# Diagonal products in place of scaled transpositions, scalar steps on ScalarE, last additions on GpSimd and an earlier last tile, in a fused two-block transformer kernel

## The reference

```python
x = layer_norm(x, emb_ln_g, emb_ln_b)
mix = concat(y_a, y_b) @ w_out
x = layer_norm(ALPHA * x + gt1 * mix, ln1_g, ln1_b)
h = x * (1.0 + sc2) + sh2
f = (silu(gate) * up) @ w_ffn_out                 # 2816 hidden features
x = layer_norm(ALPHA * x + gt2 * f, ln2_g, ln2_b)  # end of the first block
u = rms_norm(x, norm_mix_pre) @ w_in_2             # second block
x = x + rms_norm(concat(o_nsa, o_conv) @ w_out_2, norm_mix_post)
h = rms_norm(x, norm_ffn_pre)
x = x + rms_norm((gelu(g) * up) @ w_ffn_down, norm_ffn_post)
```

## Time and profile before

| | |
|---|---|
| median of 3 runs | 1548.7 us (1545.46 to 1552.2) |
| the profiled execution | 1547.24 us, of which the span is 1545.4 us |
| mean granted TensorE clock | 0.956 of full speed |
| TensorE busy | 1418.1 us, 92% of the span |
| VectorE busy | 665.0 us, 43% |
| ScalarE busy | 548.5 us, 35% |
| GpSimd busy | 486.9 us, 32% |
| HBM traffic | 95 GB/s over the span |

### The profile page before, as it was taken

The page is one execution under the profiler, slowest core; times in us unless marked ns, Lnnn a source line. Parts: engine busy times, 40 slices in busy tenths (PEclk is TensorE's granted clock), DMA queues, the critical chain, the costliest instruction groups (busy, mean ns, idle before and its releaser), DMA issues.

```text
span 1545.4 us, 22772 instructions
## 1 busy us (share of the span) xinstructions
PE 1418.1 (92%) x9466; PEld 1166.4 (75%) x9466; DVE 665.0 (43%) x1199; ACT 548.5 (35%) x800; POOL 486.9 (32%) x132
## 2 busy tenths in 40 slices
PE   4899989899789999999987899999987999998996
PEld 1688767786678888878867878888777888887885
DVE  2555665353466333320046514687244544442003
ACT  2435534233242323221124244555355343432112
POOL 1333232014324444434331231111232444433341
PEclk9899999998889999999997798999999999999998
DMA  9652255002212232323322321101121223232211
GB/s 373 167 151 83 82 201 179 35 3 80 84 47 99 101 99 92 109 82 109 109 82 104 123 69 41 56 28 56 68 83 55 94 97 106 85 109 83 95 55 54
DMA packets 24596, 147.91 MB, mean 96 GB/s; under 512 B 2700, under 2 KB 3852, under 8 KB 8880
## 3 DMA queue, kind: packets, MB, share of 16 engines
q1 hardware_dynamic: 19152, 130.96, 24.0%
q10 hardware_dynamic: 5344, 15.51, 3.7%
HBM read 141.74 MB, written 4.72 MB: 95 GB/s over the span
## 4 chain that ended last, share of the span: by engine, by line
PE 77%; DVE 12%; ACT 4%; DMA 2%; POOL 2%; issue 2%; SPq 0%; ACTq 0%; DVEq 0%; POOLq 0%
PE bank L1974 20%; PE bank L1975 20%; PE bank L1976 20%; PE bank L2232 6%; POOL weight_lo L1254 2%; PE bank L1148 2%; DVE bank L1618 2%; DMA raw<-in_weights 2%; PE bank L1068 1%; ACT weight_hi L1293 1%; PE bank L2139 1%; PE bank L1139 1%; PE bank L1130 1%; DMA w<-in_w 1%; DVE xres L1615 1%
## 5 line engine op out<-in xcount | busy, mean ns | idle before, releaser
L1254 POOL TENSOR_TENSOR weight_lo<-raw,weight_hi 128x2048 fp32r<-128x2048 f32 (+1 forms) x98 | 445.6, 4548 | 881.0 <-ACT weight_hi L1293 880.9
L1974 PE MATMUL bank<-act_hi,weight_hi 128*128 128x512 f32 (+2 forms) x1136 | 437.4, 385 | 22.0 <-POOL weight_lo L1254 8.7
L1975 PE MATMUL bank<-act_lo,weight_hi 128*128 128x512 f32 (+2 forms) x1136 | 427.6, 376 | 0.0
L1976 PE MATMUL bank<-act_hi,weight_lo 128*128 128x512 f32 (+2 forms) x1136 | 427.3, 376 | 0.0
L1293 ACT ACTIVATE weight_hi<-raw 128x2048 fp32r<-128x2048 f32 (+1 forms) x98 | 185.1, 1890 | 414.1 <-PE bank L1976 406.1
L1974 PEld LDWEIGHTS bank<-act_hi,weight_hi 128*128 128x128 f32 (+1 forms) x1136 | 218.3, 192 | 64.6 <-issue 15.5
L1976 PEld LDWEIGHTS bank<-act_hi,weight_lo 128*128 128x128 f32 (+1 forms) x1136 | 217.9, 192 | 38.8
L1975 PEld LDWEIGHTS bank<-act_lo,weight_hi 128*128 128x128 f32 (+1 forms) x1136 | 218.5, 192 | 35.1
L1974 PE MATMUL bank<-weight_hi,hid_hi 128*128 128x512 f32 x352 | 141.0, 401 | 6.8 <-DVE acc L1618 4.7
L1975 PE MATMUL bank<-weight_lo,hid_hi 128*128 128x512 f32 x352 | 140.7, 400 | 0.0
L1976 PE MATMUL bank<-weight_hi,hid_lo 128*128 128x512 f32 x352 | 140.4, 399 | 0.0
(11 more groups left out here) (352 smaller groups left out, 1749.8 us busy)
## 6 DMA issues: line engine op xcount, KB each, us to landing
raw<-in_weights SPq DMA_DIRECT2D x120, 1024.0 KB, 4.8
w<-in_w ACTq DMA_DIRECT2D x2, 2048.0 KB, 10.9
bias_rows<-grow ACTq DMA_DIRECT2D x1, 2560.0 KB
xres<-in_x SPq DMA_DIRECT2D x4, 512.0 KB, 7.0
strip<-bias_rows ACTq DMA_DIRECT2D x1, 2048.0 KB, 9.2
out<-xres SPq DMA_DIRECT2D x4, 512.0 KB, 2.6
row_a<-in_ln_g ACTq DMA_DIRECT2D x2, 512.0 KB, 4.0
row_b<-in_ln_b ACTq DMA_DIRECT2D x2, 512.0 KB, 5.1
```

The source lines that it names most:

```text
L1254: pool.tensor_tensor(wlo[i % SPLIT][:, :size], raw[n % RAW][:, :size], whi[i % SPLIT][:, :size], ALU.subtract).then_inc(lo_ready, 1)
L1974: pe.matmul(o, l[0], r[0], start=first, stop=False)
L1975: pe.matmul(o, l[0], r[1], start=False, stop=False)
L1976: return pe.matmul(o, l[1], r[0], start=False, stop=last)
```

## The change

- **Filler order.** Tile 3 of `out1_0` is done after one more filler step, and tile 3 of `out1_1` after the remaining four. Each counts its unit as used right there; `dense_rows` skips the two units.
- **h3 and h4.** `xres` itself is multiplied by a diagonal matrix `diag` of the row scales (a plain product of 128 columns). ScalarE writes the 128 by 128 diagonal from the identity where it wrote the scaled tile. All three turns now wait tile by tile: eight feature groups of the first tile, then eight of the second.
- **Scalar steps.** Adding epsilon, scaling by 1/1024 and adding the two sums go into the bias and scale of ScalarE's root, or one small ScalarE step ahead of it. In h2 the offset is made by two small ScalarE steps. VectorE's steps for them are gone, and `inverse_x` of a tile stands between the halves of the next tile's normalisation.
- **Root early.** A root on a spare column stands ahead of `mix2` and of `ff2`.
- **The end.** VectorE multiplies into `acc` and GpSimd adds to `xres`, for all but the last half of the last tile. The last tile is stored in two halves.

```diff
+    last = [[("out1", n, TT - 1, k) for k in range(2)] for n in range(2)]
+    return order + begun[:1] + last[0] + begun[1:] + last[1] + [("norm", 2, 7), ("mixer", 2), ("norm", 3, 7), ("mixer", 3)]
...
+            first, second = squares[:, 2 * t:2 * t + 1], squares[:, 2 * t + 1:2 * t + 2]
+            a.step(act.activation(first, first, ACT.Identity, bias=eps[:, 1:2], scale=1.0 / DM))
+            a.done(act.activation(rstd[:, t:t + 1], second, ACT.Sqrt, bias=first, scale=1.0 / DM), S["rms_root"])
+
+        a.step(act.activation(eps[:, 3:4], eps[:, 2:3], ACT.Sqrt))
...
+            for x in between:
+                inverse_x(e + 1, x)
...
+        def last_rows(t):
+            dve.wait_ge(S["rms_root"], TT + t + 1)
+            d.step(V.reciprocal(rstd[:, t:t + 1], rstd[:, t:t + 1]))
+            if t >= 2:
+                dve.wait_ge(S["added"], 2 * (t - 1))
+            for j in range(2):
+                name, h = ("ff2", t, j), slice(SEQ * j, SEQ * j + SEQ)
+                if (t, j) == (TT - 1, 1):
+                    stt(bank(name)[:], bank(name)[:], rstd[:, t:t + 1], row4[:, h], ALU.mult, ALU.mult)
+                    tt(xres[:, t, h], xres[:, t, h], bank(name)[:], ALU.add, sem=drain(name, "dve"))
+                else:
+                    at = DM * (t % 2) + SEQ * j
+                    stt(acc[:, at:at + SEQ], bank(name)[:], rstd[:, t:t + 1], row4[:, h], ALU.mult, ALU.mult, sem=drain(name, "dve"))
...
+        for t in range(TT):
+            for j in range(2):
+                if (t, j) != (TT - 1, 1):
+                    h, at = slice(SEQ * j, SEQ * j + SEQ), DM * (t % 2) + SEQ * j
+                    await_drained(pool, ("ff2", t, j), "dve")
+                    o.step(pool.tensor_tensor(xres[:, t, h], xres[:, t, h], acc[:, at:at + SEQ], ALU.add), S["added"])
...
+        def normalise_row(t):
+            m, r = mv[:, t, 0:1], rstd[:, t:t + 1]
+            a.step(act.activation(m, m, ACT.Copy, scale=-1.0))
+            act.wait_ge(S["inverse1"], t + 1)
+            a.step(act.activation(m, m, ACT.Copy, scale=r))
+            a.done(act.activation(xres[:, t, :], xres[:, t, :], ACT.Identity, bias=m, scale=r), S["xn_ready"])
...
-            a.done(act.activation(xn2[:, t, :], xres[:, t, :], ACT.Copy, scale=x_sums[:, t:t + 1]), S["xn3_ready"])
+            a.done(act.activation(diag[:, t, :], ident[:], ACT.Copy, scale=x_sums[:, t:t + 1]), S["xn3_ready"])
...
-                early = begun is not None and n < len(begun)
-                weights = begun[n] if early else next_unit(f"{unit}_{n}")[0]
+                if begun is not None and n < len(begun):
+                    continue
+                weights = next_unit(f"{unit}_{n}")[0]
...
+                for k in range(KC):
+                    at, x = HALF * (k % 2) + P * t, source[:, 2 * half + t, P * k:P * k + P]
+                    o = bank((stage, half, k // 2))[:, at:at + P]
+                    if stage == "h2":
+                        mm = pe.transpose(o, x, ident[:])
+                    else:
+                        mm = pe.matmul(o, x, diag[:, 2 * half + t, :], start=True, stop=True)
+                    if t and k % 2:
+                        fill((stage, half, k // 2), mm)
...
+            mm = rows_product("mix1", n, 4, begun[n], (act_hi, act_lo), t, k)
+            if (t, k) == (TT - 1, 1):
+                mm.then_inc(unit_used, 1)
```

More of the change, by code:

```diff
@@ L843, in second_act, with second_dve @@
                 act.dma_start(row4[:], src["ffn_post"].partition_broadcast(P)).then_inc(load["rows4"], 16)
-        for s in range(TT + 1):
-            squares_of_rows("ff2", 1, s, rms_t2)
-    def second_dve(dve, d, ts, tt, stt, affine_lo_half, x_mean_square, inverse_x):
+                a.step(act.activation(eps[:, 3:4], eps[:, 2:3], ACT.Sqrt))
+        for t in range(TT):
+            squares_of_rows("ff2", 1, t, rms_t2)
+    def second_dve(dve, d, ts, tt, stt, affine_lo_half, inverse_x):
         V = dve
@@ L1004, in second_dve, with add_rms @@
             tt(act_lo[:, k, :], bank(("turn_o", k))[:], act_hi[:, k, :].bitcast(F32), ALU.subtract, sem=drain(("turn_o", k), "dve"))
-        def mean_square(stage, t):
-            for j in range(2):
-                await_drained(dve, (stage, t, j), "act")
-            tt(rstd[:, t:t + 1], squares[:, 2 * t:2 * t + 1], squares[:, 2 * t + 1:2 * t + 2], ALU.add)
-            ts(rstd[:, t:t + 1], rstd[:, t:t + 1], 1.0 / DM, RMS_EPS, ALU.mult, ALU.add, sem=S["rms_ready"])
-        def add_rms(stage, e, t, row):
+        def add_rms(stage, e, t, row, between=()):
             dve.wait_ge(S["rms_root"], TT * e + t + 1)
@@ L1050, in second_dve @@
         dve.wait_ge(load["rows4"], 16)
-        for s in range(TT + 1):
-            if s < TT:
-                mean_square("ff2", s)
-            if s:
-                add_rms("ff2", 1, s - 1, row4)
+        for t in range(TT):
+            last_rows(t)
     def second_pe(pe, three, next_unit, dense_feature, dense_token, dense_rows, dense_halves, fill):
@@ L1181, in finish @@
     def finish(sp):
-        for t in range(TT):
-            await_drained(sp, ("ff2", t, 1), "dve")
+        for t in range(TT - 1):
+            sp.wait_ge(S["added"], 2 * t + 2)
             sp.dma_start(out[0, tok(t), :], xres[:, t, :]).then_inc(load["out"], 16)
-        sp.wait_ge(load["out"], 16 * TT)
+        t = TT - 1
+        sp.wait_ge(S["added"], 2 * t + 1)
+        sp.dma_start(out[0, tok(t), 0:SEQ], xres[:, t, 0:SEQ]).then_inc(load["out"], 16)
+        await_drained(sp, ("ff2", t, 1), "dve")
+        sp.dma_start(out[0, tok(t), SEQ:DM], xres[:, t, SEQ:DM]).then_inc(load["out"], 16)
+        sp.wait_ge(load["out"], 16 * (TT + 1))
     @block.sync
@@ L1665, in _ @@
         d.step(V.memset(grow[:, SEQ:], -NEG), S["future_ready"])
+        for n, value in enumerate((LN_EPS, RMS_EPS, 1.0)):
+            d.step(V.memset(eps[:, n:n + 1], value))
         d.step(V.memset(restart[:], 1.0))
@@ L1945, in second_norm @@
                 stt(b, b, mv[:, t, 0:1], row2_a[:, h], ALU.subtract, ALU.mult)
+            for x in between:
+                inverse_x(0, x)
             for j, h in enumerate(halves):
@@ L2059, in dense_rows @@
                     order = [(t, k) for t in range(TT) for k in range(2)]
-                elif n == 0 or early:
-                    tiles = (TT - 1,) if early else range(TT)
-                    order = [(t, k) for k in range(2) for t in tiles]
                 if ready is not None and n in ready:
@@ L2091, in turn_half @@
                 pe.wait_ge(ready[0], ready[1] + 2 * half + t + 1)
-            for i in range(KC // 2):
-                for k in (2 * i, 2 * i + 1):
-                    for t in range(2):
-                        at = HALF * (k % 2) + P * t
-                        mm = pe.transpose(bank((stage, half, i))[:, at:at + P], source[:, 2 * half + t, P * k:P * k + P], ident[:])
-                fill((stage, half, i), mm)
+                for k in range(KC):
[7 more added lines that the diff above has]
+                        fill((stage, half, k // 2), mm)
         def dense_halves(names, stage, source, ready):
```

79 lines of the change are left out of this document (26 added, 53 removed).

## The result

The changed kernel takes 1513.8 us (median of 4 runs, 1510.79 to 1514.91), the kernel before in the same comparison 1547.08 (4 runs, 1544.32 to 1552.2). The ratio is 0.9777 (95% interval 0.9755 to 0.9798): 2.2% faster. The forecast was 1522, the range 1513 to 1534. On its own base of 1548.7 the forecast meant 26.7 us; measured were 33.3. The direction was right and the gain too small.

What follows compares the result with a forecast made beforehand. TensorE, busy 92% of the span, was taken to bound the kernel through its work or waits. 6.4 + 2.3 + 3.1 + 8.1 + 6.3 = 26.2 us off 1547.24 gave 1521.0 profiled, 1522 for the median, range 1513 to 1534.

Steps and rivals of the forecast that it cites:

- Filler order: First output product: tile 3 done earlier, so TensorE's 4.0 us wait goes and the clock stays up; 6.4 us.
- h2: Offset steps move from VectorE to ScalarE, so VectorE's `act_lo` comes 3.0 earlier; 2.3 us gain, bounds 0 and 4.
- The 0.7 lost in h2's second half: Order tile by tile fills the first bank after 10 transpositions instead of 4, 0.7 us later for ScalarE.
- The price of a product: h3 and h4: each product against `diag` replacing a transposition takes 0.29 us, so 16 last 4.6 us.
- Products dearer: Rival: the 64 products run at half clock or four times a transposition; 7 to 10 us go, 1531; chance 0.14.
- h3: VectorE's shorter list gives 1.7 in the first half; 3.1 us in all, bounds -1.5 and 5.
- in the second half TensorE is through at 832.9: h3's second half: TensorE's own list ends at 832.9, diagonals there by 830.9 and 834.1, products to 837.5.
- the wait of 3.77 gone: h3's second half: TensorE's 3.77 us wait ahead of the transpositions disappears.
- clock kept: Rival: half clock over 820.5 to 827 and behind 429.14 goes too, 2 to 4 us more, 1517; chance 0.08.
- h4: Table load, sums and scalar addition leave the path, diagonals ready before TensorE; 8.1 us, bounds 1 and 10.
- The end: After the last product: GpSimd shares the additions, ending near 1535.7 instead of 1542.4; 6.3 us, bounds 4 and 7.

Runs made afterwards that it cites:

- experiment 5: Changed kernel, but ScalarE writes the scaled tile again and TensorE transposes it in h3 and h4, no diagonal: ratio 0.9764 to the kernel before.
- experiment 6: Changed kernel with the turns of h2, h3 and h4 bank by bank again after a wait for both tiles: ratio 0.9772 to the kernel before.
- experiment 14: Changed kernel, by banks in h4 and h2's second half, first sum's small step ahead of the second square: 1517.46 and 1518.23 us, ratios 0.9797 and 0.9810.
- experiment 2: Kernel before with the new filler order alone: 1539.83 us, ratio 0.9960.
- experiment 11: Kernel before with only the order by tiles in all three turns: 1539.95 us, ratio 0.9967.
- experiment 3: Changed kernel with the offset of h2 back on VectorE: ratio 0.9827 to the kernel before.
- experiment 8: Changed kernel with sum, scale and epsilon of `mix2` back on VectorE: ratio 0.9804 to the kernel before.
- experiment 13: Changed kernel with ScalarE's former order, and VectorE's sums, epsilons and reciprocal places, back in h3 and h4 (first block's epsilon stays on ScalarE): ratio 0.9844.

## Why the prediction was off

The gain came out 7.5 us larger in the profiled execution. One step failed, what sets the start of the turn in h3's second half; one term was mis-sized, the price of a product; 2.9 us of the 7.5 have nothing to do with the change.

**Filler order** (6.4, measured 6.9) and **h2** (2.3, measured 2.1 to 3.1): right in mechanism and size. The 0.7 lost in h2's second half is there too: from the first product to the landmark 31.34 became 32.16.

**The price of a product** (0.29, measured 0.22 to 0.23) was mis-sized, and by the reading of the earlier trace rows, not by the choice of the row. I divided its 1.16 us by four products; in it stand a longer first instruction (0.38) and the time in which the last one runs out. The last five of its eight instructions, in a window of the trace of before:

```profile
211.75 0.72 PE L2217 MATMUL bank<-wsT,pv 128*128 128x128 f32 x5
```

One instruction lasts 0.275 in this group, so they follow each other at (0.72 - 0.275) / 4 = 0.11: 0.22 for a product, as measured after. "Products dearer" was the wrong side. The rule of the page "TensorE: Matmul & The Clock Gate", section "Terms", of the Trainium skill (transpose mode four times faster for float32) does not hold here: 3.73 against 1.91 for 16 is a factor of 2.0.

**h3** (3.1, measured 4.8): here a step failed, and not only a size. Up to the first product behind the turn, 805.54 to 820.45 became 794.42 to 807.61, 1.7 less, as forecast. The failed step is the second half: I had TensorE's own list set the start of the turn ("in the second half TensorE is through at 832.9") and the wait of 3.77 gone. In its place VectorE sets it: the end of its second normalisation frees the banks. The step in the kernel before and in the changed one:

```profile
832.48 1.54 DVE L1618 SCALAR_TENSOR_TENSOR xres<-bank,rstd,row_b 128x512 f32<-128x512 f32 x2
```
```profile
819.74 1.54 DVE L1628 SCALAR_TENSOR_TENSOR xres<-bank,rstd,row_b 128x512 f32<-128x512 f32 x2
```

Before, the turn (838.42) came 4.4 us behind the end of this step (834.02), with a square, two roots and two scaled tiles between; now (821.63) it comes 0.35 behind it. TensorE's pace has no part in it, as the second trace of the changed kernel shows. There the 96 products behind the first half ran at a lower clock, and only the wait ahead of the turn shrank, from 2.28 to 0.80:

```profile
823.62 3.96 PE L2102 MATMUL bank<-diag,xres 128*128 128x128 f32 x32 [0.80 <-DVE xres L1628]
```
```profile
809.60:822.82 13.22, 13.22 (x96) 0.87 0.24 81
```

In all eight traces that hold this h3 the turn starts 20.3 us ahead of the landmark, 14.0 behind the first product, while that wait lies between 0.75 and 2.28. So the rival "clock kept" is no gain in this stretch, though it came true there as a fact (96 products in 11.7 instead of 14.2): without the diagonal (experiment 5) they took 14.2 again, at 0.79, and h3 grew by 0.5 only. My forecast meant 14.2 from the first product to the turn, by TensorE's old pace; that 14.0 came out is luck. So of the 1.7 us, 0.2 lie here, 0.5 are the price, 4.1 instead of 4.6 for the second turn, and 1.1 lie behind it, where 840.57 to 857.88 (17.3 us, at 0.89) became 16.2, at 0.97 and at 1.00 in the two traces. Only there can "clock kept" have been worth something.

**h4** (8.1, measured 10.5): every step came as forecast, and the price above was the term that was mis-sized. First half: the end of `mix2` to the next product, 8.97 (1138.20 to 1147.17) became 5.80, 3.2 less (forecast 2.4). Second half: 10.3 became 3.9, 6.4 less (forecast 5.7). Ten products at 0.06 less give 0.6 up to the first full bank, 16 give 0.9. Another 0.5 lies in the 96 products of the first half, where a wait on `weight_lo` went from 0.60 to 0.21; in the changed kernel's second trace a lower clock (0.87) takes it back. Some 0.4 is spread over the rest.

**The end** (6.3, measured 6.5): right. GpSimd's addition takes 1.28 and is hidden up to the seventh.

So of the 7.5 us between the forecast for the profiled execution (1521.0) and its time (1513.50), 1.7 lie in h3, 2.4 in h4, 0.5 in the filler, h2 and the end, 0.9 in `ff2`, and 2.0 in parts that the change doesn't touch (the start 2.6, the middle -0.6). The last two are the execution's and not the change's: in the second trace `ff2` took 125.84, as before.

**What carries h3 and h4.** The edits don't add up, since each hides behind the others. For h4's tail, step by step from the kernel before: 44.9; order by tiles 43.8 (1.1 less); with diagonal and early root 38.5 (5.3 less); with ScalarE's steps and order 35.5, or 34.5 at the higher clock (3.0 to 4.0 less). Taken away singly from the full change, early root, ScalarE's order and the reciprocals' place cost nothing there, the sums 1.6, and without the diagonal or the order by tiles it is even shorter, by 0.8 to 1.8 and by 0.8 (experiments 5, 6 and 14). For h3: order by tiles 1.4, the diagonal and early root with it nothing more, the scalar steps and their order 3.4; taken away singly, the order by tiles costs 5.8 and ScalarE's order 5.5, each by a later turn and a lower clock in it. Diagonal and early root weren't put on separately, so how the 5.3 us in h4 divide between them is open. It is open too whether h3 gains when each bank is claimed just ahead of its first use.

## What to carry to other kernels

When a tight chain of several engines is shortened, forecast its parts in order of time and expect single undone edits to show next to nothing; the sum shows only when the chain is rebuilt step by step from the old kernel. Ask of each wait which engine's list sets the start behind it: products that run faster ahead of a wait for another engine only lengthen the wait. Ask what is claimed ahead of the first instruction: a loop by tiles doesn't overlap anything while all its banks are claimed at once. And take the price of an instruction from the distance between two of them, not from the length of a short group.

## What the runs showed of the hardware

**The clock falls behind a wait in one execution and not in the next.** Behind a wait of 2.4 to 2.5 us ahead of `mix2`, the first 5 us of the changed kernel, in the two traces of it:

```profile
1079.76:1084.76 5.00, 5.00 (x15) 0.66 0.00 0
```
```profile
1080.60:1085.60 5.00, 5.00 (x22) 1.00 0.00 0
```

15 products against 22 are 7 × 0.23 = 1.6 us. The 18 traces fall into two groups there, nine with 42.5 to 42.7 us up to the turn and nine with 40.9 to 41.1. The same happens behind h4's first half, 12.06 us at 1.00 or 13.05 at 0.87 for the same 96 products. A single trace cannot tell an edit of that size there.

**VectorE and GpSimd.** A VectorE step on one column, 0.16 us elsewhere, took 2.87 to 3.28 us eleven times in seven traces: twice in each of the four that keep the old scalar steps (as in the earlier trace rows; the kernel before twice, experiments 2 and 11), and once in experiments 3, 8 and 13. Each time it began beside GpSimd's wide subtraction and ended within 0.03 us of it, as in experiment 8 at 1132.67 against 1128.06 + 4.60 = 1132.66. All are steps with two inputs in SBUF; two reciprocals on one column, with one input, took 0.16 each at 407.24 and 407.64 of the changed kernel, beside a subtraction from 406.10 to 410.71. The page "SBUF — State Buffer" of the Trainium skill, section "Who interferes with whom", says that a VectorE instruction with two SBUF inputs contends with a GpSimd instruction that reads SBUF; the traces agree.

**A plain float32 product of 128 columns** takes twice a transposition, 0.23 us against 0.12, when it stands among its like, in the kernel before (read as above) and in the changed one.
